# Four forms of the feature stages' products, chosen by ring slot, in a two-layer hybrid decoder trunk

## The reference

```python
def conv_ffn(x, w_in, w_dw, w_out):            # w_in (2048, 11264), w_out (5632, 2048)
    u = causal_dwconv(x @ w_in, w_dw)
    g, up = jnp.split(u, 2, axis=-1)
    return (jax.nn.silu(g) * up) @ w_out

def diff_attention(x, w_qkv, ...):             # w_qkv (2048, 6144)
    q, k, v = jnp.split(x @ w_qkv, 3, axis=-1)
    ...

for i in range(2):
    hn = rms_norm(h, pre_mix_g[i])
    y = conformer_conv(hn, ...) if i == 0 else diff_attention(hn, ...)
    h = h + rms_norm(y, post_mix_g[i])
    f = conv_ffn(rms_norm(h, pre_ffn_g[i]), ffn_w_in[i], ffn_w_dw[i], ffn_w_out[i])
    h = h + rms_norm(f, post_ffn_g[i])
    h = h + per_layer_embed(h, p[i], ...)
```

## Time and profile before

| | us |
|---|---|
| median of 3 runs | 2436.07 |
| lowest and highest | 2432.6, 2437.91 |
| the profiled execution: its time | 2432.6 |
| the profiled execution: its span | 2432.6 |
| PE busy | 2404.0 |
| PEld busy | 2054.3 |
| DVE busy | 1638.4 |
| ACT busy | 1238.4 |

### The profile page before, as it was taken

One profiled execution on the slowest core, in us unless ns is written; L12 is line 12 of the kernel. 1 busy time (PEld: TensorE's weight loads), 2 busy tenths in 40 slices (PEclk: granted clock), 3 DMA queues, 4 the chain that ended last, 5 costly groups with the idle time before them and its releaser, 6 DMA issues.

```text
span 2432.6 us, 38695 instructions
## 1 busy us (share of the span) xinstructions
PE 2404.0 (99%) x12312; PEld 2054.3 (84%) x12312; DVE 1638.4 (67%) x2223; ACT 1238.4 (51%) x1777; POOL 36.2 (1%) x65
## 2 busy tenths in 40 slices
PE   9999999999999999999999999999999999999998
PEld 8888778888888888888788887888888888888886
DVE  6999767777777754447755676577777777644465
ACT  3433645555555544446644455465656665444363
POOL 2000000000000000000000000000000000000000
PEclk9999999999999999999999999999999999999999
DMA  8552546556666665556575544556566656655563
GB/s 267 183 167 83 173 147 202 183 183 197 191 183 185 199 212 194 192 188 226 174 224 189 179 155 146 193 155 186 184 191 194 189 180 196 212 188 198 195 222 135
DMA packets 370941, 452.47 MB, mean 186 GB/s; under 512 B 27460, under 2 KB 279494, under 8 KB 369440
## 3 DMA queue, kind: packets, MB, share of 16 engines
q1 hardware_dynamic: 367456, 435.54, 56.1%
q0 software_dynamic: 2960, 15.02, 1.8%
q10 hardware_dynamic: 432, 0.79, 0.1%
HBM read 447.05 MB, written 4.19 MB: 186 GB/s over the span
## 4 chain that ended last, share of the span: by engine, by line
PE 83%; issue 4%; ACT 1%; DVE 1%; POOL 0%; ACTq 0%; POOLq 0%; DVEq 0%
PE ps L1592 32%; PE ps L1594 16%; PE ps L1627 11%; PE ps L1628 11%; PE ps L1629 11%; PE ps L1572 1%; PE ps L1827 0%; PE ps L1841 0%; DVE x L1037 0%; ACT w_hi L622 0%; ACT x L652 0%; DVE w_lo L1012 0%; ACT vq L781 0%; DVE h L1057 0%; PE ps L1943 0%
## 5 line engine op out<-in xcount | busy, mean ns | idle before, releaser
L1012 DVE TENSOR_TENSOR w_lo<-raw,w_hi 128x1024 fp32r<-128x1024 f32 x758 | 923.6, 1224 | 628.4 <-ACT w_hi L622 622.7
L1592 PE MATMUL ps<-x,w_hi 128*128 128x512 f32 x3328 | 1159.1, 394 | 3.2 <-issue 3.0
L622 ACT CAST w_hi<-raw 128x1024 fp32r<-128x1024 f32 x758 | 790.8, 1048 | 725.7 <-PE ps L1629 371.4
L1594 PE MATMUL ps<-x,w_lo 128*128 128x256 f32 x3328 | 928.1, 279 | 0.0
L1592 PEld LDWEIGHTS ps<-x,w_hi 128*128 128x128 f32 x3328 | 625.3, 188 | 145.9 <-issue 4.4
L1594 PEld LDWEIGHTS ps<-x,w_lo 128*128 128x128 f32 x3328 | 628.8, 189 | 0.0
L1629 PE MATMUL ps<-w_hi,mid 128*128 128x512 f32 x704 | 274.0, 389 | 0.0
L1627 PE MATMUL ps<-w_hi,mid 128*128 128x512 f32 x704 | 274.0, 389 | 0.0
L1628 PE MATMUL ps<-w_lo,mid 128*128 128x512 f32 x704 | 274.0, 389 | 0.0
L1627 PE MATMUL ps<-w_hi,x 128*128 128x512 f32 x640 | 253.8, 397 | 5.7 <-DVE x L1037 4.3
L1629 PE MATMUL ps<-w_hi,x 128*128 128x512 f32 x640 | 249.4, 390 | 0.0
(11 more groups left out here) (191 smaller groups left out, 1295.6 us busy)
## 6 DMA issues: line engine op xcount, KB each, us to landing
raw<-in_ffn_w_in SPq DMA_DIRECT2D x704, 256.0 KB, 3.1
raw<-in_ffn_w_out SPq DMA_DIRECT2D x352, 256.0 KB, 3.4
raw<-in_attn_w_qkv SPq DMA_DIRECT2D x192, 256.0 KB, 2.9
raw<-in_ple_w_gate SPq DMA_DIRECT2D x128, 256.0 KB, 3.5
wg<-in_conv_w_pw SPq DMA_DIRECT2D x112, 256.0 KB, 3.9
raw<-in_conv_w_pw SPq DMA_DIRECT2D x64, 256.0 KB, 3.6
raw<-in_attn_w_o SPq DMA_DIRECT2D x64, 256.0 KB, 3.5
wg<-in_conv_w_pw SPq DMA_DIRECT2D x32, 128.0 KB, 3.8
```

What stands on the lines that cost most here:

```text
L622: nc.scalar.copy(w_hi[:, u % RING], raw[:, u % RING]).then_inc(hi_split, 1)
L1012: nc.vector.tensor_tensor(w_lo[:, u % RING], raw[:, u % RING], w_hi[:, u % RING].bitcast(F32), ALU.subtract).then_inc(split_done, 1)
L1592: mm(ps[:, 4 * s + f], w_hi[:, u % RING, q, columns], x[:, kt].rearrange("p a t -> p (a t)"), start=kt == 0, stop=False)
L1594: ins = mm(ps[:, 4 * s + f, 0:T], w_lo[:, u % RING, q, columns], x[:, kt, 0], start=False, stop=kt == KT - 1)
```

## The change

`u % RING` now picks one of four forms for a unit of the feature stages.

- Slot 0: as before.
- Slot 1: the blocks come in the order 0 2 1 3 (a half keeps its order).
- Slot 2: the wide product is taken as two of 256 columns, with the high part of the activation and then with the rest, both into the first half of the bank. With the narrow one that makes three products of 256 columns per pair. The second half of the bank gets nothing in such a unit; what it would have got is in the first half.
- Slot 3: the narrow product adds to columns 256 to 511 of the bank.

The first unit of a chunk, whose first products start the sums, is always in slot 0.

```diff
+                def crossed(blocks):
+                    return [f for b in range(2) for f in blocks if f % 2 == b]
+
                 def product(j, blocks):
 
                     u = place[name] + n * UPC + j
                     pe.wait_ge(split_done, plus(i, per, is_split(u)))
                     for q in range(UNIT_KT):
                         kt = UNIT_KT * j + q
-                        for f in blocks:
+                        for f in (crossed(blocks) if u % RING == 1 else blocks):
                             columns = slice(P * f, P * (f + 1))
-                            mm(ps[:, 4 * s + f], w_hi[:, u % RING, q, columns], x[:, kt].rearrange("p a t -> p (a t)"),
-                               start=kt == 0, stop=False)
-                            ins = mm(ps[:, 4 * s + f, 0:T], w_lo[:, u % RING, q, columns], x[:, kt, 0],
-                                     start=False, stop=kt == KT - 1)
+                            hi, lo, last = w_hi[:, u % RING, q, columns], w_lo[:, u % RING, q, columns], kt == KT - 1
+                            if u % RING == 2:
+                                for a in range(2):
+                                    mm(ps[:, 4 * s + f, 0:T], hi, x[:, kt, a], start=False, stop=False)
+                            else:
+                                mm(ps[:, 4 * s + f], hi, x[:, kt].rearrange("p a t -> p (a t)"), start=kt == 0, stop=False)
+                            columns = slice(T, 2 * T) if u % RING == 3 else slice(0, T)
+                            ins = mm(ps[:, 4 * s + f, columns], lo, x[:, kt, 0], start=False, stop=last)
                     return ins
```

## The result

| | before | changed kernel |
|---|---|---|
| median, us | 2434.52 (4 runs) | 2459.57 (4 runs) |
| lowest to highest | 2432.6 to 2437.91 | 2457.55 to 2462.56 |
| span of the profiled execution | 2432.6 | 2460.8 |

What follows compares the result with a forecast made beforehand. TensorE's product rate was taken to bound the feature stages; slots 0 to 3 summed as 0 + 0 + 10.8 + 0 = +10.8 us, giving 2446.9 us on the median, with an 8-in-10 range of 2437 to 2453.

Steps and rivals of the forecast that it cites:

- The bound: Feature stages: the rate at which TensorE takes products sets the end; one ns per pair is 3.3 us of the kernel.
- The price of slot 2: Slot 2's 832 pairs: three narrow products, 359.7 ns against 346.7, so +13.0 ns per pair, +10.8 us.
- The cost of 13.4 ns: Feature stages: at full clock each fp32r product takes its columns' time and 13.4 ns more, so a third product adds one gap.
- the first: Slot 2: the gap belongs to the switch between operands, so the added product costs 2.4 ns, +2.0 us, 2438.1; chance 0.19.
- the third rival: Faster: narrow products in a row reach 109 ns, -15.6 us, or slots 1 or 3 shed the gap, -11.1 each; chance 0.09.
- Slot 0 keeps its code: 0: Slot 0's units: unchanged code, so no change in time, 0 us.
- the zeros of slots 1 and 3: Slot 1's bank order is worth at most 0.2 us, slot 3's early re-addition doesn't stall; each taken as 0.
- The prediction's own sign of being wrong: Forecast wrong if a narrow product inside slot 2 doesn't take 118 to 122 ns, or a slot other than 2 moves.
- The second rival: Weight loads pace slot 2, or the early re-addition in slots 2 and 3 stalls: +32 us, 2468; chance 0.09.

Runs made afterwards that it cites:

- the control: Kernel before with slot 2's triples, plus one triple in place of the fourth pair in each slot-3 unit: 2462.37 us, ratio 1.0107.
- form 1 alone: Kernel before with only the block order 0 2 1 3 in units of slot 1: 2436.81 us, ratio 1.0001.

## Why the prediction was wrong

- The bound was read rightly: TensorE's rate in the feature stages sets the end, and no wait moved.
- The price of slot 2 was right: 119.9 ns per narrow product forecast, 360 ns per triple measured, so +10.8 us of the whole. That was in part luck: 119.9 is a difference between two streams, and the exact starts in the pair stream of before give a narrow product 112 to 117 ns and a wide one 231 to 233, so no row showed what a row of narrow ones takes. The cost of 13.4 ns belongs to each product and not to the change of weights, and neither the first nor the third rival came in. The Trainium skill ("TensorE: Matmul & The Clock Gate", section "Back-to-back issue gap") gives N/2.4 + 2.5 ns as the gap of a single isolated product, and says that it leaves out the weight loads of a stream. The prediction took it for an added product in a stream; the runs of narrow fp32r products here stand at 120 ns, 13.3 above their 106.7 ns of columns.
- Slots 1 and 3 cost nothing by themselves: ratios 1.0001 and 1.0000 (0.9991 to 1.001 both), and up0's loop at 346.7 ns per pair with form 1 in it.
- The step that failed is "Slot 0 keeps its code: 0", and with it the zeros of slots 1 and 3 once slot 2 stands beside them. It took a pair's 346.7 ns for a property of its instructions. The runs showed that it is one of two steady spacings of that stream, that the triples leave the stream in the other one, and that it stays there: 2496 pairs x 6.6 ns = 16.5 us. With 10.8 that makes 27.3 us, against 28.2 between the profiled spans and 25.0 between the medians. From the first start to the last in each, the three feature stages take 1192.8 us in the changed kernel's profile and 1165.8 in that of before, 27.0 more, and the rest of the kernel 1.2 more. The prediction's own sign of being wrong, a slot other than 2 that moves, is there: a unit of slots 3, 0 and 1 takes 8 x 353.3 ns = 2.83 us and not 2.77.
- The second rival was near in size (+32 us) and wrong in its mechanism. It put the loss in slots 2 and 3, and the changed kernel and the control have slots 0 and 1 in the slow spacing as well.
- What should have been done: read the spacing in every stretch where it isn't constant, and not only as a mean over 300 us. Three units of the q and k stage's first chunk stood there with another number and the same code.

What holds the stream in its spacing isn't settled. The patterns repeat after one or two pairs (fast) and three (slow), and an extra product at one place in the pattern switches it and at another doesn't. The start of the weight load doesn't tell the spacings apart: each load starts 1 to 5 ns behind the start of the product before it, 2.7 ns on the mean in before from 400 to 700 us and 3.0 in the slow q and k loop of form 1 alone.

## What to carry to other kernels

A rate that is read off a steady stream belongs to the stream in that state and not to the instruction alone. Before an interleaved form is priced, look in the trace for stretches where the same code has another spacing, and take that spacing as a bound for all the code behind the new form. A form that is tried in one slot of four is measured together with what it does to the other three, so give each form a kernel of its own. And compare means per instruction of the untouched neighbours first (here 400 ns against 394): they show such an effect in one row.

## What the runs showed that was not expected

- In one and the same program, the same units were in the slow spacing in one execution and in the fast one in two others.
- One stream of alternating wide and narrow fp32r products, at full granted clock, has two steady spacings, 346.7 and 353.3 ns per pair (1.9%). The first has patterns of one pair or of two, the second one of three pairs.
- One added product in 128 pairs cost 11 us of 2436, and 104 triples, each moved by two pairs, were worth 17 us.
- A wide product behind eight narrow ones takes 233 ns, and the stream needs about five of them to come down to 227.
- Narrow fp32r products in a row, each with its own load, take 119 to 120 ns each for 106.7 ns of columns, in rows of 8 and of 24. In the fast pairs a narrow one takes 112 to 117.
